# One 1 MB piece of an expert's down weights held in 64 partitions and loaded by eight DMAs of 8 partitions

## The chip, the cores and the metric

The kernel runs on one core of a Trainium2 chip. The metric is the device time of one execution in microseconds (us). The core has TensorE (PE, matmuls; its weight loads are listed as PEld), VectorE (DVE), ScalarE (ACT), GpSimd (POOL) and SyncE (SP, which here only waits and issues DMAs), SBUF with 128 partitions, PSUM for matmul results, and 16 DMA engines that bring data from HBM.

## The reference

One block of a hybrid encoder on x of 256 frames by 1024, all in float32. Two token mixers and their merge come first; then a mixture of experts, top 4 of 32, each with `w_gate_up` of 1024 x 2048 (8 MB) and `w_down` of 1024 x 1024 (4 MB):

```python
    for e in range(N_EXPERTS):
        gu = t @ w_gate_up[e] + b_gate_up[e]
        gate = jnp.minimum(gu[:, :D_FF], SWIGLU_LIMIT)
        up = jnp.clip(gu[:, D_FF:], -SWIGLU_LIMIT, SWIGLU_LIMIT)
        glu = gate * jax.nn.sigmoid(SWIGLU_ALPHA * gate)
        y = ((up + 1.0) * glu) @ w_down[e] + b_down[e]
        out = out + combine[:, e:e + 1] * y
```

The result is x plus this sum, normalised.

## The kernel before

**Mixers.** The first 230 us or so are the mixers, with their own weight chunks. The rest is the experts.

**Experts.** Experts go in pairs p with i = 0, 1 (expert n = 2p + i). For a pair, the at most 64 frames that chose an expert are gathered from x2 (`gather_half`), and for each expert PE runs `gate_up` (L1491 for the bias, L1515 for the products), DVE and ACT make the activation `up` (`glu_of` L1143 to L1150, `sigmoid_of` L710), PE transposes it with four transposes (`transpose_act` L1529), ACT copies the result to SBUF as `actT` (`actT_copy` L714), and PE runs `down_bias` (L1534) and `down` (L1545). `scatter` (L1552) adds the previous expert's output to the frames' accumulators. If an expert has more than 64 frames, a second loop at the end does the rest.

**Weights.** An expert's 12 MB are 12 chunks of 1 MB: chunks 0 to 7 are gate and up, 8 to 11 down. A chunk fills 128 partitions of 8 KB. `ORDER` is the order in which PE takes the chunks; the experts go one after the other, but for the last two (30 and 31), whose down chunks come after both gate-ups. `plan()` makes the list `LOADS` of (first chunk, number of chunks, place): SBUF has 23 places of 1 MB, and a load fills 1, 2 or 4 neighbouring places (`slot`, `pair`, `quad`). Toward the end the loads get smaller: pairs for experts 28 to 31, single slots for the down weights of experts 30 and 31. From the ninth expert on the loads turn round the places from 1 up and use neither place 0 nor places 5 and 6. Place 5 was last read by PE long before expert 29.

**SP** issues all loads in the order of `LOADS`. Before each it waits until PE has finished with what lay in that place:

```python
                    sp.wait_ge(chunk_done, MIX_CHUNKS + AFTER[load] + 1)
                to = {1: slot, 2: pairs, 4: quads}[n][p]
```

The piece that changes is the load of chunks 8 and 9 of expert 29, a pair of 2 MB in places 7 and 8, issued at L361/L363's branch for pairs. It comes behind the load of chunks 6 and 7 and ahead of that of chunks 10 and 11.

**PE's down loop.** Each chunk is four products with 64 stationary columns; the two with q = 0 and q = 1 go to different halves of the PSUM bank:

```python
                        for q in range(2):
                            h = SLOTS * q
                            last = mm(to[h:h + SLOTS, :], actT[:, f % 4, f // 4, :],
                                      w[:, a * D + q * 512:a * D + (q + 1) * 512], start=False, stop=(f == KT - 1))
```

The very last load is issued in two halves (L430), and PE waits for `end_loaded` before its last four products. Behind it SP issues the load of `g_final` (L432).

Of the kernel before, what the change touches and what calls it, by code (L numbers as in the profile page):

```python
# [11 lines left out]
ACT = mybir.ActivationFunctionType  # L12
AX = mybir.AxisListType

P = 128
S, D = 256, 1024
# [3 lines left out]
N_EXP, TOP_K, FF = 32, 4, 1024  # L20
# [8 lines left out]
CHUNK = 2048  # L29
MIX_RING = 8  # L30
SLOTS = 64
ROUNDS = S // SLOTS
PAIRS = N_EXP // 2
GU_CHUNKS, DN_CHUNKS = KT, KT // 2
# [14 lines left out]
PLACE = {ec: q for q, ec in enumerate(ORDER)}  # L49
# [9 lines left out]
def plan():  # L59
    loads = [(h, 1, FIRST[h % N_PLACES]) for h in range(N_PLACES + 1 + SINGLES)]  # L60
    for turn, h in enumerate(range(N_PLACES + 1 + SINGLES, QUAD_FROM, 2)):
        loads.append((h, 2, PAIR_AT[(turn + SINGLES // 2) % len(PAIR_AT)]))
    for turn, h in enumerate(range(QUAD_FROM, ALL_CHUNKS, 4)):
        p = QUAD_AT[turn % len(QUAD_AT)]
        if h < QUAD_TO:
            loads.append((h, 4, p))
        elif h < ALL_CHUNKS - 2 * DN_CHUNKS:
            loads += [(h, 2, p), (h + 2, 2, p + 2)]
        else:
            loads += [(h + m, 1, p + m) for m in range(4)]  # L70
    return loads


LOADS = plan()
BY_HALVES = range(N_PLACES - 4, N_PLACES)
FIRST_AGAIN = range(N_PLACES, N_PLACES + 4)
AFTER, COUNT, LOAD_OF, PLACE_OF, TOTAL = [], [], {}, {}, [0] * N_PLACES
_last = {}
for _i, (_h, _n, _p) in enumerate(LOADS):
    AFTER.append(max((_last.get(_p + _m, -1) for _m in range(_n))))  # L80
    TOTAL[_p] += 2 if _i in BY_HALVES or _i in FIRST_AGAIN else 1
    COUNT.append(TOTAL[_p])
    for _m in range(_n):
        _last[_p + _m] = _h + _m
        LOAD_OF[_h + _m], PLACE_OF[_h + _m] = _i, _p + _m
# [5 lines left out]
def hybrid_block(nc, x, g_mix, w_in, conv_w, conv_b, w_rg, b_rg, w_ig, b_ig, lru_lambda, b_f,  # L91
# [3 lines left out]
    with ctx:  # L95
# [63 lines left out]
        ident = sb("ident", [P, P])  # L159
# [40 lines left out]
        slot = [alias(f"slot{i}", [P, CHUNK], F32, p) for i, p in enumerate(place_at)]  # L200
        pairs = {i: alias(f"pair{i}", [P, 2 * CHUNK], F32, place_at[i]) for i in sorted({p for _, n, p in LOADS if n == 2})}
        quads = {i: alias(f"quad{i}", [P, 4 * CHUNK], F32, place_at[i]) for i in QUAD_AT}
        spill = 7
        yo = slot[5].rearrange("p (t d) -> p t d", t=TT)


# [5 lines left out]
        def h2T_at(k):  # L212
# [13 lines left out]
        up = flat(x_sb)[:, 1024:1536]  # L226
        actT = gate.rearrange("p (j h s) -> p j h s", h=2, s=SLOTS)
# [19 lines left out]
        pj = [bank("pj0"), bank("pj1")]  # L247
        acc_pair = [ctx.enter_context(nc.psum_tensor(n, [P, 1024], F32)) for n in ("s", "pt")]
        ps, (pt, po) = ([both[:, 0:512], both[:, 512:1024]] for both in acc_pair)
        ga, gb = bank("ga"), bank("gb")  # L250
# [10 lines left out]
        loaded = [sem(f"slot{i}_loaded") for i in range(N_PLACES)]  # L261
# [8 lines left out]
        chunk_done = sem("chunk_done")  # L270
# [32 lines left out]
        selw_transposed, selwt_ready, act_transposed, actT_ready, y_ready, scattered = (  # L303
            sem(n) for n in ("selw_transposed", "selwt_ready", "act_transposed", "actT_ready", "y_ready",
                             "scattered"))
# [23 lines left out]
        def _(sp):  # L329
# [22 lines left out]
            def load_expert(load):  # L352
                h, n, p = LOADS[load]
                e, c = ORDER[h]
                if AFTER[load] < 0:
                    free_after[place_at[p]]()
                else:
                    sp.wait_ge(chunk_done, MIX_CHUNKS + AFTER[load] + 1)
                to = {1: slot, 2: pairs, 4: quads}[n][p]
                if n < 4 or c < GU_CHUNKS:  # L360
                    sp.dma_start(to[:, :], load_src(e, c, n)).then_inc(loaded[p], 16)  # L361
                else:
                    sp.dma_start(to[:, :].rearrange("p (m x) -> p m x", m=2),  # L363
                                 w_down[bass.ds(e, 1), :, :].rearrange("e (m p i) n -> p (e m) (i n)", m=2, p=P)).then_inc(loaded[p], 16)
# [44 lines left out]
            for part in range(2):  # L409
# [4 lines left out]
                for load in BY_HALVES:  # L414
                    h, _, p = LOADS[load]
                    cols = slice(part * CHUNK // 2, (part + 1) * CHUNK // 2)
                    sp.dma_start(slot[p][:, cols], load_src(*ORDER[h], 1)[:, cols]).then_inc(loaded[p], 16)
            for load in FIRST_AGAIN:
                h, _, p = LOADS[load]
# [6 lines left out]
            h, _, p = LOADS[-1]  # L426
# [73 lines left out]
        def _(act):  # L500
# [101 lines left out]
            for s in range(HEADS + 2):  # L602
# [9 lines left out]
                if s < HEADS:  # L612

                    act.wait_ge(logits_ready, s + 1)
                    for q, (lo, hi) in enumerate(((0, P), (P, 3 * P))):
                        n = 2 * (s % 2) + q
                        act.activation(L[:, s % 2, lo:hi], L[:, s % 2, lo:hi], ACT.Exp, scale=1 / math.sqrt(HD),
                                       bias=stat[:, 8 + n:9 + n], accum_out=stat[:, 12 + n:13 + n]).then_inc(exp_ready, 1)
                if s % 2 == 0 and s >= 4:
                    j = s // 2 - 2  # L620
# [80 lines left out]
            def hg_copy(p):  # L701
                act.wait_ge(gathered, p * 2 + 1)
                for k in range(KT // 2):
                    ins = act.activation(hg[:, k, :, :], ga[:, k * P:(k + 1) * P].rearrange("p (i s) -> p i s", i=2), ACT.Identity,
                                         scale=gain[:, k // 4, k % 4:k % 4 + 1])
                ins.then_inc(hga_ready, 1)
# [38 lines left out]
            for n in range(2, N_EXP - 1):  # L745
                sigmoid_of(n)
                if n % 2 and n + 1 < N_EXP:
                    hg_copy(n // 2 + 1)
                if n == N_EXP - 2:
                    actT_copy(n, actT_late, gb)  # L750
                else:
                    actT_copy(n)
                if n % 2 == 0:
                    if n:
                        act.wait_ge(scattered, TT * n)
                    selWT_copy(n // 2, ga if n == N_EXP - 2 else pj[1])
                if n < N_EXP - 2:
                    Y_copy(n)
# [6 lines left out]
            with act.If(over > 0):  # L765
                with act.Fori(1, ROUNDS) as r:
                    with act.Fori(0, PAIRS) as p:
                        pair, n = r * PAIRS + p, r * N_EXP + p * 2
# [451 lines left out]
        def _(pe):  # L1220
            mm = nc.tensor.matmul
# [12 lines left out]
            for j in range(KT):  # L1234
                for t in range(TT):
# [3 lines left out]
                    c0 = S * (j % 2) + t * P  # L1239
# [112 lines left out]
            for s in range(HEADS + 2):  # L1352
                if s < HEADS and s % 2 == 0:
# [8 lines left out]
                    j = s // 2  # L1362
# [164 lines left out]
            def transpose_act(to=pj[0]):  # L1527
                for j in range(4):
                    last = nc.tensor.transpose(to[:, j * P:(j + 1) * P],  # L1529
                                               up.rearrange("p (r i) -> p i r", i=4)[:, j, :], ident[:, :])  # L1530
                last.then_inc(act_transposed, 1)
# [4 lines left out]
            def down(i, chunk_at, actT=actT, to=gb, which=range(DN_CHUNKS), second_half=None):  # L1536
                for c in which:
                    w = chunk_at(GU_CHUNKS + c)
                    for a in range(2):
                        f = 2 * c + a  # L1540
                        if second_half and f == KT - 1:
                            second_half()
# [3 lines that stand above are left out]
                                      w[:, a * D + q * 512:a * D + (q + 1) * 512], start=False, stop=(f == KT - 1))  # L1546
                    last.then_inc(chunk_done, 1)

            def scatter(i, t, first=False, Y=Y):
                for q in range(2):  # L1550
                    h = SLOTS * q
                    last = mm(acc[t][q][:, :], selWT[h:h + SLOTS, i, t * P:(t + 1) * P], Y[h:h + SLOTS, :],  # L1552
                              start=first, stop=True, skip_group_check=True)
                last.then_inc(scattered, 1)
# [61 lines left out]
            for n in range(2, N_EXP - 1):  # L1616
                p, i = divmod(n, 2)

                def chunk_at(c):
                    return chunk_of(n, c)  # L1620

                if i == 0:
                    pe.wait_ge(hga_ready, p)
                    pe.wait_ge(onehot_ready, p + 1)
                else:
                    pe.wait_ge(selwt_ready, p + 1)
                gate_up(i, chunk_at, p if i == 0 else None)
                if p + 1 < PAIRS:
                    if i == 0:
                        pe.wait_ge(sel_ready, p + 2)  # L1630
                    else:
                        pe.wait_ge(y_ready, n)
                    gather_half(i)
                if i == 0:
                    pe.wait_ge(selw_ready, p + 1)
                    pe.wait_ge(up_ready, n + 1)
                    transpose_selW(ga if n == N_EXP - 2 else pj[1])
                pe.wait_ge(y_ready, n)
                scatter(1 - i, 0)
                pe.wait_ge(act_ready, n + 1)  # L1640
                transpose_act(gb if n == N_EXP - 2 else pj[0])
                scatter(1 - i, 1)
                if n == N_EXP - 2:
                    break
                pe.wait_ge(actT_ready, n + 1)
                if i == 1 and p + 1 < PAIRS:
                    pe.wait_ge(hgb_ready, p + 1)
                down_bias(i)
                down(i, chunk_at)
                if 20 <= n < 20 + 2 * TT:  # L1650
                    add_residual((n - 20) // 2, n % 2)
            gate_up(1, lambda c: chunk_of(N_EXP - 1, c))
# [70 lines left out]
```

## Time and profile before

| what | value |
|---|---|
| median of 3 runs | 1187.64 us (1187.42 to 1188.14) |
| the profiled execution's own time | 1187.37 us |
| its span, first to last instruction | 1185.2 us |
| outside the span | 2.2 us |
| PE busy | 1155.8 us, 98% of the span |
| DMA queue q1 (SP's loads) | 451.93 MB, 93.4% of 16 engines |
| mean TensorE clock | 0.995 of full speed |

A busy PE is one that has a matmul in flight, not one at its peak: matmuls are pipelined, so the step from one start to the next tells what one costs, not the duration shown. The DMA figures are means over 16 engines and do not say which engine is busy.

### The profile page before, as it was taken

Reading aid. Unit: us, or ns where it says so; the run is one execution under the profiler, and the core shown is the slowest. Engines: PE = TensorE matmul, PEld = TensorE weight load, DVE = VectorE, ACT = ScalarE, POOL = GpSimd, SP = SyncE. Lnnn points to the kernel's source line nnn. Section 1 sums busy time; section 2 is a strip of 40 time slices with the busy share of each in tenths; the row PEclk is TensorE's granted clock in tenths of the full one; section 3 lists DMA queues with packets and bytes.
Section 4 is the critical chain, followed back from the end, with each engine's and each line's share of the span. In section 5 each row is a group of like instructions: output and inputs, shape, how many; then the busy total and the mean of one; then the engine's idle time right before and its main releaser. Section 6 shows DMA issues by size and latency. Waiting matters only on the chain.

```text
span 1185.2 us, 14507 instructions
## 1 busy us (share of the span) xinstructions
PE 1155.8 (98%) x6326; PEld 592.8 (50%) x6326; DVE 341.3 (29%) x658; ACT 267.7 (23%) x449; POOL 23.5 (2%) x36
## 2 busy tenths in 40 slices
PE   9999999999999999999999999999999999999987
PEld 9997999996433333333343333333333333333322
DVE  6678996663211010101021110101010101010102
ACT  6767677343100010000011000000000100010002
POOL 0001110101000000000000000000000000000000
PEclk9999999999999999999999999999999999999999
DMA  9957656789999999999999999999999999999996
GB/s 319 289 201 234 224 191 213 257 306 364 425 426 426 426 429 432 431 431 428 430 431 430 428 431 431 430 430 429 430 432 427 431 429 430 431 424 429 426 424 254
DMA packets 73269, 452.93 MB, mean 382 GB/s; under 512 B 7178, under 2 KB 46450, under 8 KB 52084
## 3 DMA queue, kind: packets, MB, share of 16 engines
q1 hardware_dynamic: 73072, 451.93, 93.4%
q8 instruction: 52, 0.85, 0.3%
q14 instruction: 13, 0.11, 0.0%
q10 hardware_dynamic: 132, 0.04, 0.0%
HBM read 450.88 MB, written 1.07 MB: 381 GB/s over the span
## 4 chain that ended last, share of the span: by engine, by line
PE 75%; DMA 23%; DVE 0%; ACT 0%; issue 0%; ACTq 0%; DVEq 0%
PE pj L1515 26%; PE pj L1295 16%; DMA quad<-in_w_gate_up 16%; PE gb L1545 14%; DMA pair<-in_w_gate_up 3%; DMA slot<-in_w_down 3%; PE s L1552 2%; PE ga L1485 2%; PE pt L1552 2%; PE gb L1485 2%; PE pj L1529 1%; PE pj L1491 1%; PE pj L1266 1%; PE gb L1534 1%; PE ga L1545 1%; PE s L1366 1%
## 5 line engine op out<-in xcount | busy, mean ns | idle before, releaser
L1515 PE MATMUL pj<-quad,GL 128*64 128x512 f32 x1280 | 286.1, 603 | 13.8 <-DMA quad<-in_w_gate_up 13.7
L1143 DVE TENSOR_SCALAR x_sb<-pj 128x512 f32<-128x512 f32 x32 | 22.1, 691 | 699.1 <-PE pj L1515 699.1
L1515 PEld LDWEIGHTS pj<-quad,GL 128*64 128x64 f32 x1280 | 90.6, 139 | 199.1 <-issue 176.3
L1545 PE MATMUL gb<-quad,x_sb 128*64 128x512 f32 x640 | 141.7, 595 | 0.0
L710 ACT ACTIVATE x_sb<-x_sb 128x512 f32<-128x512 f32 x32 | 20.2, 630 | 487.5 <-DVE x_sb L1143 487.5
L1515 PE MATMUL pj<-pair,GL 128*64 128x512 f32 x576 | 126.5, 594 | 3.2 <-DMA pair<-in_w_gate_up 3.1
L1295 PE MATMUL pj<-hT_hi,w_hi 128*128 128x256 f32 x424 | 121.2, 286 | 0.0
L1295 PE MATMUL pj<-hT_hi,w_lo 128*128 128x256 f32 x424 | 119.8, 282 | 0.0
L1295 PE MATMUL pj<-hT_lo,w_hi 128*128 128x256 f32 x424 | 117.9, 278 | 0.0
L830 DVE TENSOR_TENSOR w_lo<-mix,w_hi 128x1024 fp32r<-128x1024 f32 x80 | 97.5, 1260 | 36.9 <-ACT w_hi L541 36.2
L1545 PEld LDWEIGHTS gb<-quad,x_sb 128*64 128x64 f32 x640 | 44.2, 137 | 84.9 <-issue 84.9
L541 ACT ACTIVATE w_hi<-mix 128x2048 fp32r<-128x2048 f32 x39 | 74.6, 1913 | 51.5 <-PE pj L1295 47.7
L1515 PEld LDWEIGHTS pj<-pair,GL 128*64 128x64 f32 x576 | 40.2, 137 | 84.8 <-issue 77.4
L1295 PEld LDWEIGHTS pj<-hT_hi,w_hi 128*128 128x128 f32 x424 | 79.7, 188 | 5.1 <-issue 5.1
L1295 PEld LDWEIGHTS pj<-hT_lo,w_hi 128*128 128x128 f32 x424 | 80.4, 190 | 0.0
L1295 PEld LDWEIGHTS pj<-hT_hi,w_lo 128*128 128x128 f32 x424 | 79.5, 188 | 0.0
L722 ACT ACTIVATE x_sb<-gb 128x512 f32<-128x512 f32 x30 | 17.9, 597 | 222.7 <-PE gb L1545 222.7
L1545 PE MATMUL gb<-pair,x_sb 128*64 128x512 f32 x224 | 49.6, 595 | 0.0
L1515 PE MATMUL pj<-slot,GL 128*64 128x512 f32 x192 | 42.7, 596 | 0.0
L1552 PE MATMUL s<-x_sb,GL 64*128 64x512 f32 x124 | 35.0, 641 | 0.0
L1552 PE MATMUL pt<-x_sb,GL 64*128 64x512 f32 x124 | 34.9, 639 | 0.0
L1485 PEld LDWEIGHTS ga<-GL,x 128*128 128x128 f32 x240 | 27.9, 191 | 12.2 <-issue 12.2
(353 smaller groups left out, 1105.7 us busy)
## 6 DMA issues: line engine op xcount, KB each, us to landing
quad<-in_w_gate_up SPq DMA_DIRECT2D x40, 4096.0 KB, 38.0
quad<-in_w_down SPq DMA_DIRECT2D x20, 4096.0 KB, 37.7
pair<-in_w_gate_up SPq DMA_DIRECT2D x36, 2048.0 KB, 19.7
mix<-in_w_in SPq DMA_DIRECT2D x28, 1024.0 KB, 7.1
pair<-in_w_down SPq DMA_DIRECT2D x14, 2048.0 KB, 16.8
slot<-in_w_gate_up SPq DMA_DIRECT2D x21, 1024.0 KB, 8.2
slot<-in_w_down SPq DMA_DIRECT2D x14, 1024.0 KB, 21.9
slot<-in_w_down SPq DMA_DIRECT2D x12, 512.0 KB, 7.5
```

The costliest lines, as they stand in the source:

```text
L541: act.activation(w_hi[c % 2][:, :, :], mix[c % MIX_RING].rearrange("p (k n) -> p k n", k=KT), ACT.Identity).then_inc(hi_ready, 1)
L710: act.activation(sig, gate, ACT.Sigmoid, scale=ALPHA).then_inc(sig_ready, 1)
L722: act.activation(Y, gb[:, :], ACT.Identity).then_inc(y_ready, 1)
L830: v.tensor_tensor(w_lo[c % MIX_RING][:, half, :], src[:, half, :], w_hi[c % 2][:, half, :].bitcast(F32), ALU.subtract).then_inc(ready, 1)
L1143: v.tensor_scalar(gate, pj[0][:, :], LIMIT, None, ALU.min).then_inc(gate_ready, 1)
L1266: last = mm(v_banks[pair][t][:, :], x_[:, k, t * P:(t + 1) * P], w[:, 2 * m:2 * m + 2, :].rearrange("p a n -> p (a n)"), start=(k == 0 and ...
L1295: last = mm(to, lhs, rhs, start=(k == 0 and n == 0 and (a == 0 or c != C_WO)), stop=(k == KT - 1 and n == 2), skip_group_check=(c == C_WO))
L1366: last = mm(ps[h][:, c0:c0 + n], Q[r0:r0 + HD, j, q * P:(q + 1) * P], K[r0:r0 + HD, j, 0:n], start=True, stop=True)
L1485: last = mm((ga, gb)[b][:, k % 4 * P:(k % 4 + 1) * P], x2[:, t, k * P:(k + 1) * P], sel[:, t, :, :], start=(t == 0), stop=(t == TT - 1))
L1515: last = mm(pj[q // 2][h:h + SLOTS, :], hg[:, c, i, :], w[:, q * 512:(q + 1) * 512], start=(pair == 0 and c == 0), stop=(c == GU_CHUNKS - ...
L1545: last = mm(to[h:h + SLOTS, :], actT[:, f % 4, f // 4, :], w[:, a * D + q * 512:a * D + (q + 1) * 512], start=False, stop=(f == KT - 1))
L1552: last = mm(acc[t][q][:, :], selWT[h:h + SLOTS, i, t * P:(t + 1) * P], Y[h:h + SLOTS, :], start=first, stop=True, skip_group_check=True)
```

## The change

The pair of expert 29's chunks 8 and 9 becomes two loads. Chunk 9 goes alone into place 8 as an ordinary slot. Chunk 8 goes into places 5 and 6, but only into partitions 0 to 63, with 16 KB in each: partition r holds what rows r and r + 64 of an ordinary slot would hold (u = 0, 1). It is loaded by eight DMAs, and DMA number `first` writes partitions first, first + 8, ..., first + 56. PE multiplies it 64 rows at a time: eight products instead of four. The activations that belong to rows 64 to 127 have to lie in partitions 0 to 63 as well; two more transposes and one more ACT copy make them (`actT_high`).

```diff
+LOW_EXP, LOW_PLACE, LOW_PORTS = N_EXP - 3, 5, 8
+UNEVEN = next(i for i, load in enumerate(LOADS) if load[0] == PLACE[LOW_EXP, GU_CHUNKS])
+_h, _, _p = LOADS[UNEVEN]
+LOADS[UNEVEN:UNEVEN + 1] = [(_h, 1, LOW_PLACE), (_h + 1, 1, _p + 1)]
...
-    TOTAL[_p] += 2 if _i in BY_HALVES or _i in FIRST_AGAIN else 1
+    TOTAL[_p] += LOW_PORTS if _i == UNEVEN else 2 if _i in BY_HALVES or _i in FIRST_AGAIN else 1
...
+        low = pairs[LOW_PLACE]
+        actT_high = slot[0][0:P // 2, 0:2 * P]
...
-                if n < 4 or c < GU_CHUNKS:
+                if load == UNEVEN:
+                    halves = load_src(e, c, n).rearrange("(u r) x -> r u x", u=2)
+                    for first in range(LOW_PORTS):
+                        sp.dma_start(low[first:P // 2:LOW_PORTS, :].rearrange("r (u x) -> r u x", u=2),
+                                     halves[first::LOW_PORTS]).then_inc(loaded[p], 16)
+                elif n < 4 or c < GU_CHUNKS:
...
+                if n == LOW_EXP:
+                    act.wait_ge(act_transposed, n + 1)
+                    act.activation(actT_high, pj[1][0:P // 2, 0:2 * P], ACT.Identity)
...
+            def down_low():
+                pe.wait_ge(loaded[LOW_PLACE], 16 * COUNT[UNEVEN])
+                for j in range(2):
+                    for u, rows_u in enumerate((actT[0:P // 2, j, 0, :], actT_high[:, j * P:j * P + SLOTS])):
+                        for q in range(2):
+                            h, c0 = SLOTS * q, u * CHUNK + j * D + q * 512
+                            last = mm(gb[h:h + SLOTS, :], rows_u, low[0:P // 2, c0:c0 + 512], start=False, stop=False)
+                last.then_inc(chunk_done, 1)
...
+                if n == LOW_EXP:
+                    for j in range(2):
+                        nc.tensor.transpose(pj[1][0:P // 2, j * P:(j + 1) * P],
+                                            up.rearrange("p (r i) -> p i r", i=4)[:, j, P // 2:], ident[:, :])
                 transpose_act(gb if n == N_EXP - 2 else pj[0])
...
-                down(i, chunk_at)
+                if n == LOW_EXP:
+                    down_low()
+                    down(i, chunk_at, which=range(1, DN_CHUNKS))
+                else:
+                    down(i, chunk_at)
```

## Rows read from the trace of the kernel before

**Rows 1.** The page, part 2: busy tenths and GB/s in 40 slices.

```profile
PE   9999999999999999999999999999999999999987
...
GB/s 319 289 201 234 224 191 213 257 306 364 425 426 426 426 429 432 431 431 428 430 431 430 428 431 431 430 430 429 430 432 427 431 429 430 431 424 429 426 424 254
```

**Rows 2.** The chain that ended last: start us, us, what.

```profile
1089.32 38.73 DMA pair<-in_w_gate_up
1128.05 38.35 DMA slot<-in_w_down
```

**Rows 3.** Windows at the end; last columns: PE clock, DMA share, GB/s.

```profile
1167.00:1168.00 1.00, 1.00 (x8) 0.33 (x4) 0.00 (x0) 0.90 (x1) 0.00 (x0) 1.00 0.98 401
1168.00:1168.50 0.50, 0.50 (x6) 0.10 (x2) 0.00 (x0) 0.49 (x2) 0.00 (x0) 1.00 0.48 197
...
1170.00:1170.50 0.50, 0.50 (x6) 0.21 (x4) 0.00 (x0) 0.00 (x0) 0.00 (x0) 1.00 0.62 238
...
1173.00:1173.50 0.50, 0.50 (x4) 0.14 (x2) 0.00 (x0) 0.00 (x0) 0.00 (x0) 1.00 0.50 205
...
1174.00:1174.50 0.50, 0.50 (x6) 0.12 (x2) 0.00 (x0) 0.00 (x0) 0.00 (x0) 1.00 0.10 41
```

**Rows 4.** Timeline of PE: start us, us, what, count, idle before.

```profile
1066.09 13.95 PE L1515 MATMUL pj<-pair,GL 128*64 128x512 f32 x64
1079.97 2.05 PE L1485 MATMUL ga<-GL,x 128*128 128x128 f32 x16
...
1082.39 1.13 PE L1552 MATMUL s<-x_sb,GL 64*128 64x512 f32 x4
1083.45 0.75 PE L1529 MATMUL pj<-ident,x_sb 128*128 128x128 f32 x4
...
1113.26 0.50 PE L1534 MATMUL gb<-bdn,onehot 128*128 128x512 f32 x1
1113.69 7.09 PE L1545 MATMUL gb<-pair,x_sb 128*64 128x512 f32 x32
...
1121.37 7.09 PE L1515 MATMUL pj<-pair,GL 128*64 128x512 f32 x32
1129.29 3.65 PE L1515 MATMUL pj<-pair,GL 128*64 128x512 f32 x16 [0.83 <-DMA pair<-in_w_gate_up]
1134.18 3.65 PE L1515 MATMUL pj<-pair,GL 128*64 128x512 f32 x16 [1.24 <-DMA pair<-in_w_gate_up]
...
1143.34 14.28 PE L1515 MATMUL pj<-pair,GL 128*64 128x512 f32 x64
...
1166.53 1.94 PE L1545 MATMUL ga<-slot,x_sb 128*64 128x512 f32 x8 [0.41 <-DMA slot<-in_w_down]
...
1169.46 5.55 PE L1545 MATMUL ga<-slot,x_sb 128*64 128x512 f32 x24
```

**Rows 5.** Timeline of all engines, the same columns: ACT's copies.

```profile
1109.77 1.12 ACT L704 ACTIVATE GL<-ga,vec 128x128 f32<-128x128 f32 x4
...
1112.30 0.60 ACT L714 ACTIVATE x_sb<-pj 128x512 f32<-128x512 f32 x1 [1.40 <-PE pj L1529]
```

**Rows 6.** The page, part 3: DMA queues, packets, MB, share.

```profile
q1 hardware_dynamic: 73072, 451.93, 93.4%
...
q10 hardware_dynamic: 132, 0.04, 0.0%
```

**Rows 7.** Windows in two stretches of the mixers: 128-partition loads, then 32-partition ones.

```profile
20.00:22.00 2.00, 2.00 (x19) 2.00 (x19) 1.21 (x2) 2.00 (x6) 0.00 (x0) 1.00 1.09 365
...
232.50:234.30 1.80, 1.80 (x18) 1.80 (x17) 1.80 (x2) 0.00 (x0) 0.00 (x0) 1.00 1.06 220
```

**Rows 8.** Timeline of SP: its DMA issues.

```profile
1065.54 0.33 SPq L361 DMA_DIRECT2D pair<-in_w_gate_up  x1
1069.79 3.76 SPq L361 DMA_DIRECT2D pair<-in_w_down  x2
...
1115.67 25.20 SPq L361 DMA_DIRECT2D slot<-in_w_down  x7
```

## Prediction

> **What bounds the kernel now.** I read the page first, then the windows of the end, then the timelines of PE and SP there. In the page the reader is to see that both PE and the transfers are full: PE shows nines and the loads 424 to 432 GB/s from the eleventh slice to the last but one [rows 1]. The chain that ended last decides between them: its last 77 us before the final products are DMAs, a pair of 38.7 us and a slot of 38.4 us from issue to landing [rows 2]. So near the end the loads' stream sets the pace. The queue is that deep, and what is issued a few us earlier or later lands when its turn comes.
>
> The windows of the end tell more. The 16 DMA engines move 401 GB/s at a share of 0.98 until 1168, and then the share falls at once to 0.48 and is 0.50 still at 1173.5, with 0.10 after 1174 [rows 3]. Eight engines' worth of work goes on for about 6 us after the other half has none left. One engine of the first half is late too: 0.62 until 1170.5, against 0.50 at 1173. So the halves are not level: about seven engines finish near 1168.0 to 1168.8, one near 1170.5, eight near 1173.5 to 1174.5. An ordinary load gives each engine the same bytes, and the last half decides.
>
> PE is almost as tight. A gate_up without waits takes 13.95 us for 64 matmuls [rows 4], or 6.98 for 32 and 0.218 for one. For expert 30 the first 32 start at 1121.37 and the next 16 at 1129.29, a wait of 7.92 - 6.98 = 0.94; the last 16 at 1134.18, a wait of 4.89 - 3.49 = 1.40. Expert 31's takes 14.28, which is 0.33 more than 13.95. Then 0.41 at 1166.53, and in the last 24 matmuls 5.55 - 24 x 0.218 = 0.32. After expert 29's down, PE waits for loads 0.94 + 1.40 + 0.33 + 0.41 + 0.32 = **3.4 us**. This is all that earlier loads can give, and it is also what pays for PE's added work.
>
> **What the change costs PE.** A down chunk takes 7.09 / 4 = 1.77 us: 8 MATMUL records, two for each of four products. `down_low` has 8 products with 512 columns each, 16 records, half the rows. Half the rows save nothing: time goes by columns. At 0.22 each that is 3.5 us, so +1.76 [rows 4]. The nearest row with 64 rows is `scatter`, four records in 1083.45 - 1082.39 = 1.06; at that rate 16 take 4.24, so +2.5, the upper bound. I take +1.8, since q = 0 and 1 still alternate between the column halves as in the row of L1545. Two more transposes: the four at 1083.45 take at most 0.75, so +0.35. ACT's added copy is 64 x 256; its rows are 0.28 for 128 x 128 (1.12 / 4) and 0.60 for 128 x 512 [rows 5], say 0.35. `actT_copy` stands behind it on ACT, and PE's bias waits for that; it ended at 1112.90 and the bias started at 1113.26, so 0.36 of the copy is covered and I count +0.1 (0 to 0.25). Nothing else queues behind it but `Y_copy`, 7 us later. Sum **+2.2 us on PE**, 2.0 to 3.1. It lies before expert 30's gate_up, so the 3.4 us of waits take it up: if loads were no limit, PE would end 3.4 - 2.2 = 1.2 us earlier.
>
> **What it costs SP.** Eight issues for one. Issues of loads took 0.33 here, and 1.8 to 4.2 each when SP was held at full queues (the last seven slots: 25.20 us for 7 [rows 8]). 8 x 0.35 = 2.8 us fits between the load ahead, at 1065.54, and 1069.79, when SP got the old place from PE; the new place is free, so the eight start at once. Even held for 10 us, the loads behind it (chunk 9, chunks 10 and 11, expert 30) have over 25 us of queue ahead. Cost nothing; if that cover were gone, as much as the hold.
>
> **What it does to the stream.** Does a DMA with 8 rows run on 8 engines? ACT's small loads answer. Five of 8 rows, one of 2 and one of 32 make 132 packets on q10 [rows 6]. With a packet for each row and a 4-byte one for each engine used, 5 x (8 + 8) + (2 + 2) + (32 + 16) = 132. So 8 rows use 8 engines; the 1 MB gives 128 KB to each of eight instead of 64 KB to each of 16. At 430 / 16 = 26.9 GB/s, 64 KB is 2.45 us: the eight get +2.45 and the others -2.45. The same reading gives q1 8 x (16 + 8) + (128 + 16) - (128 + 16) = 192 packets more.
>
> Which eight? No row says. If they are those that end early, the last half ends 2.45 us sooner and the early ones have 5 to 6 us to spare; I give this three in four. The Trainium skill, "DMA: Bandwidth & Descriptors", section "Why a DMA increments its semaphore by 16 and not by 1", says that a DMA on k engines from SP takes the lowest-numbered k. Whether these are the early ones here, it does not say. Its "Rules for kernel authors" speak against the form: a first dimension below 16 confines a DMA to that many engines.
>
> How fast do the eight write? Loads of 32 neighbouring partitions ran at 220 GB/s with every engine busy (share 1.06), against 365 for 128 partitions with packets no larger, and 430 with large ones [rows 1, 7]. The destination limits: 32 neighbours offer half the ways into SBUF that 128 do, eight of 27 GB/s, thus one for each four neighbours, and each way serves four more partitions outside those 32. The new DMAs write partitions first, first + 8, ..., first + 56: in each 32 they touch every second group of four, four ways. If partitions 32 to 63 have ways of their own, that is eight, and the 1 MB takes 4.9 us at 215 GB/s; if they share those of 0 to 31, it is four, and it takes 9.8 us at 107. All eight DMAs have the same two engines meet at each way. The rows leave it open; I take the shared case at about 0.7, since an engine writes eight partitions of every ordinary load and two groups 32 apart are as near a pair as any. Then the eight engines get 2.45 + 4.9 = +7.35 us. The Trainium skill, "SBUF — State Buffer", section "Door 1: The DMA port swizzle", says that partitions 32 apart share a port and lists 0 to 3 with 32 to 35; by it the four-way case holds. The 220 GB/s row agrees with its figure for 32 partitions (189 to 218); no row here shows 64.
>
> **The sum.** Early engines end at 1168.0 to 1168.8 plus 7.35: 1175.3 to 1176.2. The ninth (1170.5) starts the piece 2 us behind the engine it meets and then shares less, so it ends with them, not at 1177.9. The old last half ends near 1172. Loads therefore end at about 1175.6 instead of 1174.5, **+1.1 us**, the early engines now last. PE's limit (-1.2) stays behind this. The tail after the last product is unchanged. Span 1185.2 + 1.1 = 1186.3, this execution 1187.37 + 1.1 = 1188.5; the median is 0.27 above the profiled one, so 1188.7. Forecast **1188.6 us**, its own range 1187.4 to 1190.7 (the ninth engine not helped: 1177.9 - 1174.5 = +3.4 at most).
>
> **Rivals.** (1) *Full rate*: the 1 MB at 215 GB/s. The late half ends 2.45 sooner, the ninth engine at 1172.95 (-1.55); PE's 1.2 is the smaller gain. -1.2, so 1186.4 (1185.8 to 1187.3). For it: nothing shows the sharing. (2) *The wrong half, slower*: the eight are those that end last. Then +7.35 on the last half, 1195.0; at full rate +2.45, 1190.1. It decides from the first byte, since that half has no lead. For it: the trace does not name engines. (3) *PE*: if products of 64 rows and 64 columns did not overlap in pairs, 8 x 4 x 0.218 = 7.0 against 1.76 is +5.2; with 0.45 for the rest less 3.4, +2.3, 1189.9. Against it: L1545's pairs overlap, L1485's matmuls, which fill all 128 stationary columns, take 2.05 / 16 = 0.13 for 128 moving ones, or 0.51 for 512, where L1545 needs 0.22. (4) *Nothing*: the eight DMAs spread over all engines. Then PE's 2.2 is hidden in its waits: 1187.6.
>
> **Chances.** A measurement of this kernel tells about 0.2%, 2.4 us, from no change: 1185.3 to 1190.0. Forecast 0.50 (slower by over that 0.10, same 0.40); full rate 0.23 (faster 0.03, same 0.20); wrong half 0.17 (0.13 at 1195, 0.04 at 1190, half of these slower); PE 0.04 (slower half); nothing and others 0.06 (faster 0.02). Faster 0.05, same 0.67, slower 0.28. The range 1185.6 to 1191.2 leaves out 1195 and a little at both ends, under 2 in 10.
>
> **What would show it.** q1 with 73264 packets. In the windows of the end, a share near 1 until about 1171 and then no long step at 0.5 (forecast), or a half step of 1 us at 1171 (rival 1), or a step longer than now (rival 2). Around 1099 to 1109, where the piece moves, the forecast wants 300 to 350 GB/s where the slices now stand at 424 and more, with the share still 1. PE's down of expert 29 about 1.8 us longer, and the waits in expert 30's gate_up smaller at first. The prediction is wrong if the eight engines are the late ones, or if anything lets the last half start its loads later.

## The result, and the profile after

The changed kernel takes **1198.24 us** (median of 4 runs, 1197.82 to 1198.71) against 1187.53 for the kernel before in the same measurement: ratio 1.0088, 95% interval 1.0076 to 1.01. It is 10.7 us slower, where +1.1 us was forecast and 1191.2 was the range's upper end. The profiled execution took 1197.82 us, its span 1195.6.

The page, part 2, GB/s in 40 slices, and of part 3 the queue of the loads:

```profile
GB/s 317 286 200 236 218 201 214 261 304 364 426 427 427 429 426 432 431 428 431 431 427 432 429 429 428 429 431 427 434 426 432 426 431 429 431 427 376 370 424 225
...
q1 hardware_dynamic: 73264, 451.93, 93.3%
```

The number of packets is the one that was foreseen, so the DMAs do run on eight engines each. Two slices stand at 376 and 370 GB/s, where there were 429 and 426 [rows 1]; in the experts' part the others are as before, up to the last, in which the stream ends. A slice is 1195.6 / 40 = 29.9 us, so about (53 + 56) x 29.9 = 3.3 MB were not moved in them, 7.6 us of the whole stream. The windows show where (PE and its count first, the last three columns are PE clock, DMA share, GB/s):

```profile
1090.00:1096.00 6.00, 6.00 (x30) 1.98 (x28) 0.00 (x0) 0.60 (x1) 0.00 (x0) 1.00 1.01 429
1098.00:1100.00 2.00, 2.00 (x12) 0.72 (x10) 0.00 (x0) 0.00 (x0) 0.00 (x0) 1.00 1.08 291
1100.00:1104.00 4.00, 3.21 (x16) 0.92 (x14) 0.00 (x0) 0.00 (x0) 0.00 (x0) 1.00 1.03 223
1104.00:1108.00 4.00, 1.21 (x6) 0.14 (x2) 0.00 (x0) 0.00 (x0) 0.00 (x0) 1.00 0.95 217
1108.00:1110.00 2.00, 0.00 (x0) 0.00 (x0) 0.00 (x0) 0.00 (x0) 0.00 (x0) 0.97 1.05 229
1110.00:1114.00 4.00, 3.38 (x8) 1.01 (x10) 0.00 (x0) 0.00 (x0) 0.00 (x0) 0.50 1.03 236
1114.00:1116.00 2.00, 2.00 (x8) 0.67 (x6) 0.00 (x0) 0.00 (x0) 0.00 (x0) 0.50 0.99 369
1116.00:1118.00 2.00, 2.00 (x13) 0.82 (x10) 0.67 (x2) 0.00 (x0) 0.00 (x0) 0.82 0.93 377
...
1175.00:1178.00 3.00, 2.69 (x15) 0.81 (x13) 0.00 (x0) 0.60 (x1) 0.00 (x0) 1.00 0.88 362
1178.00:1180.00 2.00, 2.00 (x12) 0.62 (x8) 0.00 (x0) 1.49 (x2) 0.00 (x0) 1.00 0.51 209
1180.00:1182.00 2.00, 2.00 (x12) 0.49 (x8) 0.00 (x0) 0.00 (x0) 0.00 (x0) 1.00 0.20 74
1182.00:1186.00 4.00, 4.00 (x20) 1.06 (x18) 0.00 (x0) 0.00 (x0) 0.00 (x0) 1.00 0.11 42
```

The DMA share stays at 1 while the rate falls to 217 to 236 GB/s. The share says that no engine is idle; the rate says that each moves half of what it did. If only eight were slowed to half, the rate would be 8 x 26.9 + 8 x 13.4 = 322. A mean over 16 engines could also be eight at full speed and eight nearly still, 8 x 26.9 = 215. The packets in the trace rule that out: of those of 16 KB that start from 1101 to 1107 on q1 the shortest takes 987 ns and the median 1246, where in the kernel before they take 611 to 624, median 613, in the same stretch. None of them goes at full speed. So **all 16** run at about half rate, from 1098.5 or so to 1114: some 16 us, where the forecast had 9.8 us on eight. From the rows, 1098 to 1118 moved 291 x 2 + 223 x 4 + 217 x 4 + 229 x 2 + 236 x 4 + 369 x 2 + 377 x 2 = 5236 KB instead of 20 x 427 = 8540, 3.3 MB or **7.7 us**. (Below, what windows "lose" is always this: the missing bytes over the 427 GB/s of the undisturbed stream.) At the end the long step at 0.5 [rows 3] has gone; a tail of 0.11 to 1186 stands in its place, 2 engines of 16.

PE shows the forecast's own part, and what it didn't foresee (start us, us, what, count, idle before; the last row is SP's, the eight issues):

```profile
1101.56 3.65 PE L1529 MATMUL pj<-pair,GL 128*64 128x512 f32 x16 [0.79 <-DMA pair<-in_w_gate_up]
1110.62 6.66 PE L1529 MATMUL pj<-pair,GL 128*64 128x512 f32 x16 [5.42 <-DMA pair<-in_w_gate_up]
...
1120.34 0.44 PE L1666 MATMUL pj<-ident,x_sb 128*64 128x128 f32 x2
...
1122.67 1.08 PE L1569 MATMUL gb<-pair,x_sb 64*64 64x512 f32 x4
...
1126.25 1.94 PE L1559 MATMUL gb<-slot,x_sb 128*64 128x512 f32 x8
...
1145.38 3.65 PE L1529 MATMUL pj<-pair,GL 128*64 128x512 f32 x16 [2.64 <-DMA pair<-in_w_gate_up]
...
1180.45 5.53 PE L1559 MATMUL ga<-slot,x_sb 128*64 128x512 f32 x24
...
1066.28 9.46 SPq L369 DMA_DIRECT2D pair<-in_w_down  x8
```

`down_low` runs from 1122.67 to 1126.25, 3.58 us: 1.8 more than a chunk, as forecast. But the load *ahead* of the piece (issued at 1065.91, before the eight) is late already, and PE stands still for 5.42 us in expert 29's gate_up, before any changed instruction of its own. The last 24 products start at 1180.45 instead of 1169.46 [rows 4]: +11.0.

### The profile page after: what moved, and what is told of

It reads as the page before. It is cut to its first block, busy times and chain, and to the rows that moved or that the text cites. A ratio compares the mean times of both kernels' runs of the same rounds, so it can differ in the third digit from the quotient of the medians.

```text
span 1195.6 us, 14536 instructions
## 1 busy us (share of the span) xinstructions
PE 1161.0 (97%) x6336; PEld 594.7 (50%) x6336; DVE 341.0 (29%) x658; ACT 268.0 (22%) x450; POOL 24.9 (2%) x36
## 3 DMA queue, kind: packets, MB, share of 16 engines
q1 hardware_dynamic: 73264, 451.93, 93.3%
## 4 chain that ended last, share of the span: by engine, by line
PE 72%; DMA 27%; DVE 0%; ACT 0%; issue 0%; DVEq 0%; POOL 0%; POOLq 0%; ACTq 0%
PE pj L1529 23%; DMA quad<-in_w_gate_up 20%; PE pj L1309 16%; PE gb L1559 13%; DMA pair<-in_w_gate_up 4%; DMA slot<-in_w_down 3%; PE gb L1499 2%; PE s L1575 2%; PE pt L1575 2%; PE ga L1499 1%; PE pj L1543 1%; PE pj L1280 1%; PE pj L1505 1%; PE gb L1548 1%; PE pj L1241 1%; PE ga L1559 1%
## 5 line engine op out<-in xcount | busy, mean ns | idle before, releaser
L1529 PE MATMUL pj<-pair,GL 128*64 128x512 f32 x576 | 129.5, 606 | 8.8 <-DMA pair<-in_w_gate_up 8.8
L1559 PE MATMUL gb<-pair,x_sb 128*64 128x512 f32 x208 | 46.1, 595 | 0.0
```

The costliest lines, as they stand in the source:

```text
L1529: last = mm(pj[q // 2][h:h + SLOTS, :], hg[:, c, i, :], w[:, q * 512:(q + 1) * 512], start=(pair == 0 and c == 0), stop=(c == GU_CHUNKS - ...
L1559: last = mm(to[h:h + SLOTS, :], actT[:, f % 4, f // 4, :], w[:, a * D + q * 512:a * D + (q + 1) * 512], start=False, stop=(f == KT - 1))
```

## The experiments

Eleven kernels ran, in three groups. Changes of time are against the runs of the kernel before that were made with the same group: 1188.21 us (first group, four kernels), 1187.75 (second, four), 1187.74 (third, three). Code is shortened: `.then_inc(...)` is left out. A "way" is, as in the prediction, one of the entries into SBUF through which DMA engines write, each serving groups of four neighbouring partitions.

**First group: what in the new load does it?** Three candidates: the destination in partitions 0 to 63, the 8-row form, the order of the source rows.

`e4_plain`: the load stands at its new place, as one DMA of 128 partitions; PE's work is the old one.

```
-  for first in range(LOW_PORTS): (8 DMAs into low[first:64:8, :])
+  sp.dma_start(slot[p][:, :], load_src(e, c, n))
```

> Chunk 8 of expert 29 is a load of its own into the free place 5, but as one ordinary DMA over 128 partitions, and PE multiplies it as before: the new list of loads without the eight DMAs and without the 64-row work. All theories expect 1187.5 us, within 1 us of the kernel before, with 420 to 430 GB/s between 1095 and 1115. If it is slow, the new place or the order of the loads is the cause.

Measured: 1187.90 us, ratio 0.9999 (0.9989 to 1.0008). The split into two loads and the new place cost nothing.

`e3_spread16`: the same, but as 16 DMAs of 8 rows, 16 apart, over all 128 partitions.

```
+  for first in range(16):
+      sp.dma_start(slot[p][first:P:16, :], load_src(e, c, n)[first::16])
```

> As the plain one, but the 1 MB comes by sixteen DMAs of 8 rows, 16 rows apart, into all 128 partitions. So all 1 MB still goes through eight engines, and the work on PE is the old one. Theory destination (writes confined to partitions 0 to 63 halve every engine): the rate stays near 430 GB/s, the eight engines get 2.45 us more and the others 2.45 us less; as two of the eight seem to be among the engines that end last, the end is 2.4 us later, 1190.0 us. Theory form (eight-row DMAs slow all engines) and theory source (rows read at large even steps): 210 to 250 GB/s for about 16 us again and 1195 to 1199 us.

Measured: 1198.31 us, ratio 1.0085 (1.0068 to 1.0102): nearly all of the loss (10.1 of 10.7 us), with none of the new PE work and not kept to partitions 0 to 63. "Destination" falls as I had put it.

`e1_one64`: the changed kernel with `LOW_PORTS = 1`: one DMA of 64 rows.

> The changed kernel, but with the 1 MB for partitions 0 to 63 loaded by one DMA of 64 rows, so by all 16 engines. Theory destination: half rate while it moves, 5 us or more at about 215 GB/s, all engines 2.5 us later, 1190 us; the eight-engine imbalance is gone. Theories form and source: full rate, and with the 64-row work hidden in PE's waits 1187 to 1188 us.

Measured: 1195.91 us, ratio 1.0062 (1.0046 to 1.0079). So it is not the number of DMAs nor their 8 rows either. All three candidates had this kernel at 1187 to 1190, so none of them stands as it was put. The time is 7.7 us over its own kernel before, 3.0 less than the changed kernel's 10.7. The windows of the stretch lose more, though, (185 + 165 + 255) x 6 / 427 = 8.5 us against 7.7, so the difference can't be put down to the 2.45 us of uneven bytes alone. Its windows, and those of `e4_plain` behind it:

```profile
1098.00:1104.00 6.00, 4.52 (x22) 1.35 (x20) 0.00 (x0) 0.00 (x0) 0.00 (x0) 1.00 0.99 242
1104.00:1110.00 6.00, 2.06 (x10) 0.43 (x6) 0.00 (x0) 0.00 (x0) 0.00 (x0) 0.99 1.05 262
1110.00:1116.00 6.00, 5.40 (x14) 1.70 (x16) 0.00 (x0) 0.00 (x0) 0.00 (x0) 0.50 1.00 172
```

```profile
1098.00:1104.00 6.00, 6.00 (x30) 1.86 (x26) 0.00 (x0) 0.00 (x0) 0.00 (x0) 1.00 1.01 427
1104.00:1110.00 6.00, 5.01 (x27) 2.16 (x26) 0.98 (x2) 0.25 (x1) 0.00 (x0) 1.00 1.01 425
```

`e7_source`: each of the eight DMAs reads 8 neighbouring rows of the source and writes rows 8 apart (the output is not the reference's, since rows change places).

> The changed kernel, but each of the eight DMAs reads 8 neighbouring rows of the weights (16 KB apart) instead of rows 128 KB apart; the rows land in the wrong partitions, so expert 29's output is not the reference's. Theory source: full rate, and only the eight-engine shift is left, about 1190 us. Theories destination and form: 1198 us as the changed kernel, with 210 to 250 GB/s for 16 us.

Measured: 1199.28 us, ratio 1.0097 (1.0081 to 1.0114). The order of the source rows is not the cause.

**Second group: which rows an engine writes.** What the slow forms share is that row and engine don't go together as in an ordinary load. The Trainium skill, "DMA: Bandwidth & Descriptors", section "The descriptor swizzle", says that in a load of 128 partitions each engine writes two groups of four partitions, 32 apart, and only those, engines 0 to 7 in partitions 0 to 63. A DMA of 8 rows on engines 0 to 7 keeps to that map if its rows are r, r + 4, ..., r + 28. That can be tested without trusting the page:

`e2_stride4`: the changed kernel, the eight DMAs with rows 4 apart.

```
-  low[first:P // 2:LOW_PORTS, :]
+  r0 = first // 4 * 32 + first % 4
+  low[r0:r0 + 29:4, :]            (source rows alike)
```

> The changed kernel, same bytes, same eight DMAs of 8 rows, same PE work, but a DMA's eight rows stand 4 apart instead of 8 (rows r, r+4, ..., r+28 with r = 0 to 3 and 32 to 35). Theory 'foreign': in an ordinary load of 128 rows each engine writes two groups of four neighbouring partitions, 32 apart, and only those; when an engine writes partitions of another's groups, all 16 run at half rate until the last such piece has landed. With rows 4 apart the eight engines write their own groups, so 424 GB/s or more all through 1098 to 1114, and only the uneven bytes stay: +2.45 us on the eight, two of which are late ones, so 1190 us (1189 to 1191). Theory 'form': any DMA of 8 rows slows the others, whatever its rows; then 200 to 290 GB/s over 1098 to 1114 again and 1198 us.

Measured: **1189.93 us**, ratio 1.0017 (1.0008 to 1.0026). Same bytes, same number and form of DMAs, same PE work: 8.5 us of the 10.7 are gone. Windows, where the piece moves and at the end:

```profile
1098.00:1114.00 16.00, 14.97 (x76) 5.93 (x73) 2.99 (x5) 1.66 (x5) 0.00 (x0) 1.00 1.01 425
```

```profile
1168.00:1170.00 2.00, 1.54 (x8) 0.29 (x4) 0.00 (x0) 0.41 (x1) 0.00 (x0) 1.00 0.87 348
1170.00:1172.00 2.00, 1.39 (x8) 0.57 (x8) 0.00 (x0) 1.66 (x3) 0.00 (x0) 1.00 0.88 360
1172.00:1174.00 2.00, 2.00 (x10) 0.50 (x8) 0.00 (x0) 0.01 (x1) 0.00 (x0) 1.00 0.55 225
1174.00:1176.00 2.00, 2.00 (x12) 0.54 (x10) 0.00 (x0) 0.00 (x0) 0.00 (x0) 1.00 0.14 55
1176.00:1178.00 2.00, 2.00 (x12) 0.56 (x10) 0.00 (x0) 0.00 (x0) 0.00 (x0) 1.00 0.13 51
```

Full rate throughout, which agrees with the page's map. The end tells, by inference, which engines carry the piece: 14 of 16 still work at 1168 to 1172, where half were done [rows 3], so most of the early ones have got the added 2.45 us; and two go on alone to 1178, so two of the late ones have got it as well.

`e8_shift`: rows 4 apart again, but starting at 4, 5, 6 and 7, so that each engine writes its neighbour's group; four DMAs only, half of the bytes stay out.

> As the changed kernel, but only four of the eight DMAs are issued (half of the 1 MB stays out, so the output is not the reference's), with rows 4 apart, starting at 4, 5, 6 and 7: the same form and stride as in the run with rows 4 apart, only shifted by one group of four partitions, so that each engine writes its neighbour's group. 'Foreign': half rate for the transfer of 64 KB at each engine (4.9 us) and the 6 us spread between the engines, 11 us in all, 5.5 us lost; the eight carry as many bytes as in an ordinary load, so 1193 us (1192 to 1194.5). 'Form', or if only the stride of 8 was at fault: full rate with stride 4, 1187 to 1188 us; if every 8-row DMA slows the rest, half of the loss, 1191.6.

Measured: 1192.73 us, ratio 1.0038 (1.0025 to 1.0052). A shift by four partitions brings the half rate back: 262 GB/s over 1098 to 1110, so (427 - 262) x 12 / 427 = 4.6 us lost, and +5.0 at the end.

`e5_half`: the changed kernel with four of its eight DMAs (rows 8 apart; half of the bytes stay out).

> The changed kernel with the first four of its eight DMAs alone (rows 8 apart; half of the 1 MB stays out, so the output is not the reference's). If the half rate lasts as long as any engine still has such a piece, it lasts 4.9 us of transfer and 6 us of spread between early and late engines: 11 us at half rate, 5.5 us lost, 1193 us. If the loss is proportional to the bytes so moved: 8.2 / 2 = 4.1 us, 1191.6.

Measured: 1194.96 us, ratio 1.0058 (1.0044 to 1.0072). Two rows, `e8_shift` and `e5_half`:

```profile
1098.00:1110.00 12.00, 6.94 (x32) 1.98 (x30) 0.00 (x0) 0.00 (x0) 0.00 (x0) 0.96 1.00 262
```

```profile
1098.00:1110.00 12.00, 6.61 (x32) 1.99 (x30) 0.00 (x0) 0.00 (x0) 0.00 (x0) 0.96 1.01 246
1110.00:1114.00 4.00, 4.00 (x10) 0.97 (x10) 0.00 (x0) 0.00 (x0) 0.00 (x0) 0.50 1.01 346
```

The windows of `e5_half` lose (181 x 12 + 81 x 4) / 427 = 5.8 us, with half of the bytes of the changed kernel, which loses 7.7. In proportion to the bytes it would be 3.9. Transfer plus the engines' 6 us of spread, at half rate, gives (4.9 + 6) / 2 = 5.5 and (9.8 + 6) / 2 = 7.9, which fits both. It is a rule of thumb and does not hold everywhere: `e8_shift` lost 4.6 where it gives 5.5, and `e1_one64` lost 8.5 where 4.9 us of transfer (1 MB over eight ways, as in the prediction) would give 5.5 as well. The time of `e5_half` itself, +7.2, is 1.4 above the windows' loss; I can't place that.

`e6_early`: the kernel before, with another 1 MB load, one that lands near 317 us, as 16 DMAs of 8 rows, 16 apart.

> The kernel before, but another ordinary 1 MB load, the last slot load of the first part (it lands near 317.5 us), goes as 16 DMAs of 8 rows, 16 apart, over all 128 partitions; all the rest is as before. The engines land there within 2 us of each other, not 6. If the half rate lasts for transfer plus spread: 9.8 + 2 = 12 us, some 210 to 290 GB/s over 314 to 328 and back above 420 after that; 5.9 us lost plus 2.45 for the uneven bytes, 1193 to 1196 us if the loads have no slack there. If the length doesn't depend on the spread: 16 us of half rate, as with the late load, and 1198. If the loads have slack that early, the windows still show the stretch but the end stays at 1188 to 1190.

Measured: 1194.91 us, ratio 1.0055 (1.004 to 1.007).

```profile
314.00:318.00 4.00, 4.00 (x21) 1.23 (x19) 1.98 (x3) 1.46 (x5) 0.00 (x0) 1.00 0.80 240
318.00:320.00 2.00, 2.00 (x12) 0.62 (x10) 0.69 (x1) 0.20 (x1) 0.00 (x0) 1.00 0.50 115
320.00:322.00 2.00, 2.00 (x12) 0.72 (x10) 0.00 (x0) 0.00 (x0) 0.00 (x0) 1.00 0.77 168
322.00:324.00 2.00, 1.98 (x11) 0.79 (x7) 0.00 (x0) 0.67 (x2) 0.00 (x0) 1.00 1.08 197
324.00:326.00 2.00, 2.00 (x18) 1.88 (x18) 0.00 (x0) 0.53 (x1) 0.00 (x0) 1.00 0.91 176
326.00:328.00 2.00, 2.00 (x9) 0.77 (x9) 2.00 (x7) 0.00 (x0) 0.00 (x0) 1.00 0.91 377
```

Two things to see. The row at 318 has a share of 0.50 and 115 GB/s: eight engines alone, 14.4 GB/s each. They are slow although the other eight move nothing, so the eight are enough. Here I had missed that the queue isn't deep yet: SP issues the 16 DMAs at 0.6 us each, and the other eight run out of work. And PE is busy throughout and waits for nothing here, yet the end comes 7.2 us later. The windows' loss over 314 to 328 is (14 x 427 - 240 x 4 - 2 x (115 + 168 + 197 + 176 + 377)) / 427 = 6.9 us. So this stream, which sets the end, hands on what it loses 870 us before the end too. The uneven bytes do not show: with 2.45 us for a late engine among the eight it would be 6.9 + 2.45 = 9.4. Whether the idle time of the other eight already holds them, no run separates.

**Third group: sharing, or another's partitions as such? And what does PE cost?** The first two edit the kernel before, a 2 MB pair load whose bytes move near 377 us, where the engines are nearly level; of it, only four DMAs of 8 rows are issued (1.5 MB stay out).

```
+  for r in range(4, 8):
+      rows = slice(r, r + 29, 4)        # e9_early_shift
+      rows = slice(r - 4, r + 53, 8)    # e10_early_share
+      sp.dma_start(to[rows, :], load_src(e, c, n)[rows])
```

> The kernel before, but of one ordinary 2 MB pair load early in the run (issued near 370 us, its bytes move near 376 to 382 us, where the 16 engines stand within 2.5 us of each other) only four DMAs of 8 rows are issued, rows 4 apart starting at 4, 5, 6 and 7: every one of the eight engines writes its neighbour's group of partitions, no two of the eight the same; 1.5 MB of the load stay out, so the output is not the reference's. Theory 'sharing': half rate only while two engines write the same way into SBUF. With the engines in step that is only at the start and the end of the piece, so 2 to 3.5 us below 424 GB/s. Theory 'foreign': an engine that writes another's partitions slows all, shared or not: twice 2.45 us and the spread, about 7 us at 210 to 290 GB/s.

> As the run with the shifted early piece, same place and bytes, but the four DMAs' rows stand 8 apart starting at 0, 1, 2 and 3, so that by the map of groups two of the eight engines meet in each way all the time. Both theories: 4.9 us and the spread, about 7 us at 210 to 290 GB/s. If this one is slow for long and the shifted one is not, sharing is the cause; if both are, writing foreign partitions is.

Measured: 1186.38 us, ratio 0.9988 (0.9979 to 0.9997), and 1187.86 us, ratio 1.0003 (0.9994 to 1.0012). First `e9_early_shift`, then `e10_early_share`:

```profile
377.00:378.00 1.00, 1.00 (x8) 0.75 (x7) 0.63 (x2) 0.00 (x0) 0.00 (x0) 1.00 1.05 262
378.00:379.00 1.00, 1.00 (x11) 1.00 (x10) 0.83 (x3) 0.91 (x3) 0.00 (x0) 1.00 0.80 328
379.00:380.00 1.00, 1.00 (x7) 0.41 (x5) 0.90 (x2) 0.76 (x3) 0.00 (x0) 1.00 1.03 410
380.00:381.00 1.00, 0.99 (x6) 0.56 (x4) 1.00 (x3) 0.00 (x0) 0.00 (x0) 1.00 1.06 295
381.00:382.00 1.00, 1.00 (x5) 0.30 (x4) 1.00 (x6) 0.60 (x1) 0.00 (x0) 1.00 0.93 360
```

```profile
377.00:378.00 1.00, 1.00 (x11) 1.00 (x10) 0.91 (x2) 0.18 (x1) 0.00 (x0) 1.00 1.07 229
378.00:379.00 1.00, 1.00 (x12) 0.88 (x10) 0.83 (x2) 1.00 (x4) 0.00 (x0) 1.00 1.02 213
379.00:380.00 1.00, 1.00 (x5) 0.26 (x4) 0.90 (x3) 0.48 (x2) 0.00 (x0) 1.00 0.94 197
380.00:381.00 1.00, 0.99 (x8) 0.79 (x8) 1.00 (x5) 0.12 (x1) 0.00 (x0) 1.00 1.12 246
381.00:382.00 1.00, 1.00 (x5) 0.24 (x3) 1.00 (x6) 0.48 (x1) 0.00 (x0) 1.00 0.78 229
```

With two engines to a way, five windows in a row stand at 197 to 246. With one engine to each way, though a foreign one, the rate dips at the start (262), is back at 410 in the middle, where all eight are inside the piece, and dips again on leaving (295). The packets of 16 KB say the same: over 377 to 382 the shortest of the shared form takes 779 ns, median 1218; in the shifted form some keep the full-speed 611 ns, and the median is 669. So it is sharing, not foreign partitions as such; that a shared way arises only while one of two neighbours is in the piece and the other not is my explanation of the dips. They are longer than the 2 to 3.5 us that I had expected, and shallower. Over 377 to 382 the shifted form loses 1.1 us of transfer (1655 instead of 2135 KB) and the shared one 2.4 (1114 KB); the times differ by 1.5.

The times come out if a late engine among the eight sets the end. It still gets 64 KB of this load instead of 128, so it saves 2.45 us (one of the other eight saves 4.9): -2.45 + 1.1 = -1.3 and -2.45 + 2.4 = -0.1, against -1.4 and +0.1 measured. PE is not the limit, since it still waits for a load in its last products; and in `e9_early_shift` two engines (share 0.12) go on alone near the end. Two rows of `e9_early_shift`, then one of `e10_early_share`:

```profile
1171.00:1173.00 2.00, 1.84 (x10) 0.39 (x8) 0.00 (x0) 0.00 (x0) 0.00 (x0) 1.00 0.12 49
1172.61 1.08 PE L1550 MATMUL ga<-slot,x_sb 128*64 128x512 f32 x4 [0.16 <-DMA slot<-in_w_down]
```

```profile
1171.88 3.65 PE L1550 MATMUL ga<-slot,x_sb 128*64 128x512 f32 x16 [1.10 <-DMA slot<-in_w_down]
```

`e11_pe_only`: the changed kernel's PE and ScalarE work, its chunk loaded as one ordinary load of 128 partitions (`down_low` reads 64 of its rows twice, so the output is not the reference's).

> The changed kernel's PE and ScalarE work (two more transposes, one more copy, eight products of 64 rows for the chunk) with the chunk loaded as one ordinary load of 128 partitions at its new place; the products read the wrong rows, so the output is not the reference's. If PE's 2.2 us are hidden in its waits for loads, as forecast: 1187.5 to 1188.3, no change. If the 2.2 us of the run with rows 4 apart (1189.9) are PE's and not the uneven bytes': 1189.5 to 1190.

Measured: 1187.69 us, ratio 1.0003 (0.9994 to 1.0012). PE's 2.2 us are hidden, as forecast, and the 2.2 us of `e2_stride4` are not PE's; its end windows give them to the uneven bytes.

## Why the prediction was wrong, step by step

- *The loads' stream bounds the end, the halves are not level, PE's waits take up 3.4 us*: right. `e11_pe_only` shows no cost of PE's added work, and `down_low` took its 3.58 us. *SP's eight issues cost nothing, and the new place neither*: right (`e4_plain`, `e2_stride4`), though the issues took 9.46 us and not 2.8; the cover of over 25 us held.
- *Eight rows run on eight engines, +2.45 us for each*: right. The packets are 73264, and `e2_stride4`, with nothing but the uneven bytes, is at +2.2.
- ***"Then the eight engines get 2.45 + 4.9 = +7.35 us"*: this step failed.** That ways are shared and the rate is half was right, and I had said "with every engine busy". I then let the other eight run on at full speed. The runs show all 16 at about half, 217 to 236 GB/s at a share of 1 instead of the 300 to 350 that I had named, with no 16 KB packet under 987 ns over 1101 to 1107. So the lead of the early engines paid for nothing: everyone lost the time.
- *Its length, 9.8 us*: too short; it was some 16. By rows 3 the engines are up to 6 us apart at the end, so they probably reach the piece that far apart too, and an engine inside it meets one that is still, or again, at ordinary loads. Transfer plus spread gives (9.8 + 6) / 2 = 7.9 us lost, against 7.7 in the windows; it is an estimate made after the result was known, and `e1_one64` does not fit it. I had used the spread as a reserve; here it is a cost.
- *The eight are the early ones (three in four), or the wrong half*: neither. By the end windows of `e2_stride4` they are most of the early ones and two of the late. These two decide: 7.7 + 2.45 = 10.2, measured 10.7; the same sum is 2.2 too high for `e6_early`. Rival 2's 1195.0 at half rate is 3.2 short of the changed kernel, since it slows only eight engines too; its 1190.1 at full rate is what `e2_stride4` (1189.9) did, for its reason.
- *The sum and the range*: +1.1 forecast, +10.7 measured. The range left out 1195 and everything above it, since no case had the others slowed.

The cause in one sentence: rows 8 apart make two engines meet in each way into SBUF, and as long as that lasts the whole queue goes at about half rate, the transfer ahead included. Shown are the loss with rows 8 apart, its absence with rows 4 apart on the ordinary map, and the difference between the shifted and the shared form; which engine writes which partition is inferred from these, since the trace names no engine. The Trainium skill, "DMA: Bandwidth & Descriptors", section "Back-pressure in remote DMA", says that a saturated destination port clogs the path back to the source engines and to others that share the path. It says so of transfers between cores; the 16 slowed engines here look the same within one. Why engines whose own groups nobody else writes are held back as well is not settled by these runs; that sentence of the Trainium skill would explain it, and no run isolates it.

PE's clock made PE later in between: after the 5.42 us without work the granted clock is 0.50 of full, the lower of the two levels (1.2 of 2.4 GHz), until about 1116, and 16 matmuls take 6.66 us instead of 3.65. The end is set by the loads all the same: PE waits 2.64 us for them later, at 1145.

No version here beats the kernel before. The form at full rate, `e2_stride4`, still gives two late engines 2.45 us more. `e9_early_shift` has 1.5 MB less to load and is no version of it.

## What to carry to other kernels

Before a load is cut into pieces with few rows, work out which engine writes which partitions: rows 4 apart, each engine in its own groups, kept this queue at 425 GB/s; rows 8 apart halved it for some 16 us. A misplaced small transfer is not paid by its own bytes alone (1 MB, 2.45 us here), but by everything in flight beside it (7.7 us here). Read DMA share and GB/s together: here a share of 1 at half the rate was contention, and half the share at half the rate, in the end windows, was missing work. And where eight engines "have time", check that the work goes to those eight; by the end windows of `e2_stride4`, two of them had none.

## What the hardware showed that I had not expected

- All 16 engines at about half rate (217 to 236 instead of 429 GB/s; 16 KB packets at a median of 1246 instead of 613 ns) while only eight have the odd piece, and also in the load issued ahead of it.
- One DMA of 64 partitions, with even bytes on all 16 engines, harms the stream for longer: 242, 262 and 172 GB/s over 18 us, the last below half, and +7.7 us in the end.
- Eight engines alone with the odd piece move 115 GB/s (share 0.50): 14.4 GB/s each, though the other eight move nothing; what holds them must be shared among the eight.
- A shift by four partitions turns a transfer at the full 425 GB/s into one at 262 where the engines stand apart; where they are nearly level it costs 1.1 us.
